# A block of two networks on one core: first projection in three passes of rounded parts, convolution taps spread over the stage and the heads of retention

## The reference, cut to what matters

```python
h = _rmsnorm(x, norm_g[0, 0]) * (1.0 + scale_m) + shift_m     # mod = silu(c) @ ada_w + ada_b
proj = h @ w_in                                                # (256, 1024) @ (1024, 3072)
a_val, a_gate, q, k, v, g = split(proj)                        # six parts of 512 columns
a = a_val * sigmoid(a_gate)
a = depthwise_conv(a, conv_w)                                  # 31 taps, 512 channels
a = silu(_layernorm(a + conv_b, cln_g, cln_b))
q, k = _rotary(q), _rotary(k)
r = silu(g) * _head_rmsnorm(_retention_bidir(q, k, v))         # 4 heads of 128
mix = concatenate([a, r]) @ w_out
```

## Time and profile before

| | us |
|---|---|
| median of 3 runs | 1404.34 (1403.9 to 1406.63) |
| the profiled execution | 1400.26 |
| its span in the profile | 1398.5 |

### The profile page before, as it was taken

The page is one execution under the profiler, slowest core; times in us unless marked ns, Lnnn a source line. Parts: engine busy times, 40 slices in busy tenths (PEclk is TensorE's granted clock), DMA queues, the critical chain, the costliest instruction groups (busy, mean ns, idle before and its releaser), DMA issues.

```text
span 1398.5 us, 21667 instructions
## 1 busy us (share of the span) xinstructions
PE 1208.0 (86%) x9250; PEld 1070.8 (77%) x9250; DVE 784.0 (56%) x1328; ACT 518.7 (37%) x857; POOL 164.5 (12%) x129
## 2 busy tenths in 40 slices
PE   5899888879979998658999999788798799887797
PEld 3688566668868887357899999788786698776697
DVE  1177312875554466775566543489776445467545
ACT  2112312211210006424455534434465535357634
POOL 0111100100000000010000000156454100041000
PEclk8999989989989998868899999889998799998899
DMA  9977659658866883899455556234332054342141
GB/s 294 354 250 242 212 125 264 208 191 279 315 228 216 150 289 114 288 248 137 136 179 184 183 192 194 65 103 135 112 105 91 31 190 142 94 131 78 61 136 45
DMA packets 203204, 244.36 MB, mean 175 GB/s; under 512 B 27173, under 2 KB 187557, under 8 KB 198885
## 3 DMA queue, kind: packets, MB, share of 16 engines
q1 hardware_dynamic: 187528, 182.24, 42.8%
q0 software_dynamic: 11280, 42.78, 10.3%
q10 hardware_dynamic: 4300, 17.96, 3.3%
HBM read 224.16 MB, written 18.81 MB: 174 GB/s over the span
## 4 chain that ended last, share of the span: by engine, by line
PE 65%; DVE 17%; DMA 6%; ACT 5%; SPq 3%; issue 3%; ACTq 0%; POOL 0%; DVEq 0%
PE ps L1285 17%; PE ps L1278 10%; PE ps L1280 10%; PE ps L1282 10%; PE ps L1333 2%; DVE ada_w L2353 2%; PE ps L1363 2%; PE ps L1306 2%; DMA ring<-in_w_glu_b 1%; DMA ada_w<-in_ada_w 1%; SPq L684 1%; PE ps L1699 1%; PE ps L1767 1%; DVE ring_rounded L1889 1%; DMA more<-in_ada_w 1%
## 5 line engine op out<-in xcount | busy, mean ns | idle before, releaser
L1278 PE MATMUL ps<-sq_rounded,w_high_rounded 128*128 128x256 f32 x960 | 283.6, 295 | 27.4 <-DVE ring_rounded L1889 8.8
L1282 PE MATMUL ps<-sq_rounded,ring_rounded 128*128 128x256 f32 x960 | 276.4, 288 | 0.0
L1280 PE MATMUL ps<-hT_rounded,w_high_rounded 128*128 128x256 f32 x832 | 239.0, 287 | 0.0
L1889 DVE TENSOR_TENSOR ring_rounded<-ring,w_high_rounded 128x1024 fp32r<-128x1024 f32 x152 | 186.6, 1270 | 88.2 <-ACT w_high_rounded L811 88.1
L1278 PEld LDWEIGHTS ps<-sq_rounded,w_high_rounded 128*128 128x128 f32 x960 | 190.1, 198 | 37.9 <-issue 31.3
L811 ACT ACTIVATE w_high_rounded<-ring 128x1024 fp32r<-128x1024 f32 x176 | 175.9, 1049 | 101.4 <-PE ps L1282 95.0
L1285 PE MATMUL ps<-hT,ring 128*128 128x256 f32 x832 | 188.3, 385 | 5.9 <-ACT hT L876 3.2
L1282 PEld LDWEIGHTS ps<-sq_rounded,ring_rounded 128*128 128x128 f32 x960 | 189.4, 197 | 0.0
L1285 PEld LDWEIGHTS ps<-hT,ring 128*128 128x128 f32 x832 | 157.7, 192 | 34.6 <-issue 13.3
L1280 PEld LDWEIGHTS ps<-hT_rounded,w_high_rounded 128*128 128x128 f32 x832 | 164.2, 197 | 0.3
L1278 PE MATMUL ps<-more_rounded,w_high_rounded 128*128 128x256 f32 x448 | 126.0, 281 | 1.6 <-issue 1.4
(11 more groups left out here) (377 smaller groups left out, 1829.1 us busy)
## 6 DMA issues: line engine op xcount, KB each, us to landing
ring<-in_w_fc SPq DMA_DIRECT2D x64, 1024.0 KB, 5.5
ada_w<-in_ada_w POOLq DMA_DIRECT2D x27, 1024.0 KB, 7.7
ring<-in_ssm_in_w SPq DMA_DIRECT2D x20, 1024.0 KB, 5.3
ada_more<-in_ada_w POOLq DMA_DIRECT2D x13, 1024.0 KB, 7.7
ring<-in_w_in SPq DMA_DIRECT2D x12, 1024.0 KB, 8.1
we_dram<-we_t ACTq DMA_DIRECT2D x8, 1024.0 KB, 5.5
ca_dram<-more ACTq DMA_DIRECT2D x8, 1024.0 KB, 8.0
ring<-we_dram SPq DMA_DIRECT2D x8, 1024.0 KB, 4.9
```

Source lines behind the costliest of these rows:

```text
L1278: nc.tensor.matmul(out, high[:, k, columns], x_high, start=start, stop=False, skip_group_check=True)
L1280: nc.tensor.matmul(out, high[:, k, columns], x_low, start=False, stop=False, skip_group_check=True)
L1282: last = nc.tensor.matmul(out, low[:, k, columns], x_high, start=False, stop=stop, skip_group_check=True)
L1889: nc.vector.tensor_tensor(rounded(w), w, w_high[:, c % 2, ks], ALU.subtract)\
```

## The change

The first projection joins the split phases. ACT rounds and DVE lowers each of its twelve blocks; the shift is folded into the split of the activations (ACT writes the rounded part to sq, DVE the rest to hT, in the helper `split_shifted`, which is taken over from phase fc1_1); blocks 8 and 9 get a form of their own, `project_tokens_split`, which waits for both halves of the lowered block. ACT rounds block 0, and DVE lowers it, ahead of the norm. DVE's taps are cut up: of 31, the first 24 are spread three at a time over eight turns of a loop that first lowers a block and in turns 1 to 4 also rotates; the last seven (LATE_TAPS) stand behind the decays of the four heads, 1, 2, 2 and 2. Counters of later waits are moved accordingly. The hunks with those counters alone are left out here.

```diff
@@ -51,6 +51,7 @@
 NCH = T // L
 WIN = (2 * L - 1) * GC
 PI = 3.1415925
+LATE_TAPS = 7
 S5_AT_FC1 = (1, 4, 7, 10, 13)
 MODULATION_AT_FC1 = (7,)
 SINGLE = 1.5 * 2 ** 23
@@ -176,11 +177,11 @@
 
 
 
-SPLIT_LO = {"glu": "vector", "fc1_1": "vector", "fc2_1": "vector", "xbc": "gpsimd", "z": "vector",
+SPLIT_LO = {"w_in": "vector", "glu": "vector", "fc1_1": "vector", "fc2_1": "vector", "xbc": "gpsimd", "z": "vector",
             "ssm_out": "vector", "ple_gate_0": "vector", "q": "vector", "gate": "vector",
             "attn_out": "vector", "ple_gate_1": "vector"}
 
-SPLIT_SETS = (("glu", 4), ("fc1_1", 8), ("fc2_1", 16), ("xbc", 8), ("ssm_out", 16), ("ple_gate_0", 8), ("q", 8),
+SPLIT_SETS = (("w_in", 8), ("glu", 4), ("fc1_1", 8), ("fc2_1", 16), ("xbc", 8), ("ssm_out", 16), ("ple_gate_0", 8), ("q", 8),
               ("attn_out", 8), ("ple_gate_1", 8))
 SET_BASE = {name: sum(n for _, n in SPLIT_SETS[:i]) for i, (name, _) in enumerate(SPLIT_SETS)}
 
@@ -805,7 +806,10 @@
                     c = split_next[0]
                     b = split_order[c]
                     act.wait_ge(w_here[b % RING], here[b])
-                    act.wait_ge(blocks_done, split_order[c - 2] + 1 if c >= 2 else first_block["glu"] - 2 * (1 - c))
+                    if b in (first_block["glu"], first_block["glu"] + 1):
+                        act.wait_ge(blocks_done, b - 2 + b - first_block["glu"])
+                    elif c >= 2:
+                        act.wait_ge(blocks_done, split_order[c - 2] + 1)
                     for half in range(2):
                         ks = slice(4 * half, 4 * half + 4)
                         nc.scalar.activation(w_high[:, c % 2, ks], ring[:, b % RING, ks], ACT.Copy)\
@@ -889,7 +893,10 @@
             for p in range(PIECES // 2):
                 act.wait_ge(ada0_parts, p + 1)
                 nc.scalar.activation(mix_flat[:, 512 * p:512 * p + 512], PS[p][:, :], ACT.Copy).then_inc(ada0_copied, 1)
-            shift(0, 0, SHIFT_M)
+            round_to(first_block["w_in"] + 1)
+            for k in range(DT):
+                act.wait_ge(hn_ready, k + 1)
+                round_tiles(sq[:, k], hT[:, k], mod(0, SHIFT_M, k))
 
 
             for j in range(2):
@@ -1305,6 +1312,22 @@
                     for k in range(KB):
                         last = nc.tensor.matmul(ps[:, i], lhs[:, k, P * i:P * i + P], w[:, k],
                                                 start=(k == 0), stop=(k == KB - 1))
+                last.then_inc(blocks_done, 1)
+
+            def project_tokens_split(phase, n, x_high, x_low):
+
+                ps = pair(start_unit(phase, n))
+                b = first_block[phase] + n
+                high, low = w_high[:, split_place[b] % 2], rounded(ring[:, b % RING])
+                pe.wait_ge(w_low_vector, 2 * split_low[b][1])
+                for i in range(TT):
+                    for k in range(KB):
+                        t_high, t_low = (rounded(x[:, k, P * i:P * i + P]) for x in (x_high, x_low))
+                        nc.tensor.matmul(ps[:, i], t_high, high[:, k], start=(k == 0), stop=False,
+                                         skip_group_check=True)
+                        nc.tensor.matmul(ps[:, i], t_high, low[:, k], start=False, stop=False, skip_group_check=True)
+                        last = nc.tensor.matmul(ps[:, i], t_low, high[:, k], start=False, stop=(k == KB - 1),
+                                                skip_group_check=True)
                 last.then_inc(blocks_done, 1)
 
             def project_deep(phase, n, kblocks, x, arrived=None):
@@ -1398,18 +1421,18 @@
 
 
             def h_arrived(i):
-                return lambda k: pe.wait_ge(h_ready, 8 * i + k + 1)
+                return lambda k: pe.wait_ge(h_ready, 8 * (i - 1) + k + 1)
 
             pe.wait_ge(x_ready, 4)
             pe.wait_ge(tables_here, 32)
             for n in range(8):
-                project("w_in", n, (hT,), h_arrived(0) if n == 0 else None)
+                project("w_in", n, (sq, hT), split_arrived("w_in") if n == 0 else None)
                 modulation(PIECES + n)
             for n in range(8, 10):
-                project_tokens("w_in", n, hT)
+                project_tokens_split("w_in", n, sq, hT)
                 modulation(PIECES + n)
             for n in range(10, 12):
-                project("w_in", n, (hT,))
+                project("w_in", n, (sq, hT))
                 modulation(PIECES + n)
 
...
@@ -1950,17 +1973,33 @@
                                                              op0=ALU.mult, op1=ALU.add)
                     ins.then_inc(x_ready, 1)
 
+            def split_shifted(phase, i, layer, which):
+                dve.wait_ge(rstd_ready, i + 1)
+                for k in range(DT + 2):
+                    if k < DT:
+                        nc.vector.scalar_tensor_tensor(out=hT[:, k], in0=xT[:, k], scalar=gains[:, i, k:k + 1],
+                                                       in1=rstd[:, :], op0=ALU.mult, op1=ALU.mult).then_inc(hn_ready, 1)
+                    if k >= 2:
+                        j = k - 2
+                        dve.wait_ge(a_high, SET_BASE[phase] + j + 1)
+                        nc.vector.scalar_tensor_tensor(out=rounded(hT[:, j]), in0=hT[:, j],
+                                                       scalar=mod(layer, which, j), in1=rounded(sq[:, j]),
+                                                       op0=ALU.add, op1=ALU.subtract).then_inc(a_low, 1)
+
+            lower_to(first_block["w_in"] + 1)
             modulation(0)
             gain(0)
-            normed(0, lambda k: gains[:, 0, k:k + 1])
+            split_shifted("w_in", 0, 0, SHIFT_M)
 
 
             nc.vector.memset(apad[:, :, 0:PAD], 0.0)
             nc.vector.memset(apad[:, :, PAD + T:], 0.0)
             for j in range(2):
+                lower_to(first_block["w_in"] + 2 * j + 2)
                 dve.wait_ge(sg_ready, j + 1)
                 ps = unit("w_in", 2 * j + 1)
                 nc.vector.tensor_tensor(apad[:, 2 * j:2 * j + 2, PAD:PAD + T], ps, sgate, ALU.mult).then_inc(a_ready, 1)
+                lower_to(first_block["w_in"] + 2 * j + 3)
             dve.wait_ge(a_ready, 2)
 
             def taps(first, last):
@@ -1990,10 +2029,12 @@
                 link(nc.vector.tensor_tensor(b, b, table("rope_sin").unsqueeze(1).to_broadcast([P, 2, T]), ALU.mult))
                 nc.vector.tensor_tensor(a, a, b, ALU.add).then_inc(qk_ready, 1)
 
-            taps(0, 14)
-            for j in range(4):
-                rotate(j)
-            taps(14, TAPS)
+            early = TAPS - LATE_TAPS
+            for n in range(8):
+                lower_to(first_block["w_in"] + n + 6)
+                taps(early * n // 8, early * (n + 1) // 8)
+                if 1 <= n <= 4:
+                    rotate(n - 1)
 
 
             def decayed(h):
@@ -2015,6 +2056,7 @@
 
             for h in range(HEADS):
                 decayed(h)
+                taps(early + LATE_TAPS * h // HEADS, early + LATE_TAPS * (h + 1) // HEADS)
                 if h >= 1:
                     gated(h - 1)
...
@@ -2273,16 +2315,7 @@
                     ins = nc.vector.scalar_tensor_tensor(out=xT[:, k], in0=glu_prod[:, i], scalar=mod(1, GATE_M, k),
                                                          in1=xT[:, k], op0=ALU.mult, op1=ALU.add)
                 ins.then_inc(x_ready, 1)
-            dve.wait_ge(rstd_ready, 4)
-            for k in range(DT + 2):
-                if k < DT:
-                    nc.vector.scalar_tensor_tensor(out=hT[:, k], in0=xT[:, k], scalar=gains[:, 3, k:k + 1],
-                                                   in1=rstd[:, :], op0=ALU.mult, op1=ALU.mult).then_inc(hn_ready, 1)
-                if k >= 2:
-                    j = k - 2
-                    dve.wait_ge(a_high, SET_BASE["fc1_1"] + j + 1)
-                    nc.vector.scalar_tensor_tensor(out=rounded(hT[:, j]), in0=hT[:, j], scalar=mod(1, SHIFT_F, j),
-                                                   in1=rounded(sq[:, j]), op0=ALU.add, op1=ALU.subtract).then_inc(a_low, 1)
+            split_shifted("fc1_1", 3, 1, SHIFT_F)
             for n in range(17):
                 if n < 16:
                     lower_to(first_block["fc1_1"] + n + 2)
```

More of the change, by code:

```diff
@@ L1558, in _ @@
                         if jq == 0:
-                            pe.wait_ge(h_ready, 8 * 2 + k + 1)
+                            pe.wait_ge(h_ready, 8 + k + 1)
                         last = nc.tensor.transpose(PS[2 * kh + jq][:, P * i:P * i + P],
@@ L2212, in _ @@
                 if b == 0:
-                    dve.wait_ge(h_ready, 8 * 3)
+                    dve.wait_ge(h_ready, 8 * 2)
                 nc.vector.tensor_copy(u_in[:, 16 * b:16 * b + 16].rearrange("p g s -> p (g s)"), PS[b][:, :])\
```

## The result

The changed kernel takes 1419.07 us, median of 4 runs (1414.76 to 1426.88), against 1404.12 before: the ratio is 1.0122, 95% interval 1.0088 to 1.0156. It is slower, as forecast, but by 15 us in the medians and 17 by the ratio, three to four times the 4.35 us of the sum, and outside the range.

The account below looks back on a forecast made before the run. PE was taken to bound the first projection, with DVE taking over after the change; +0.6 us at retention's entry and +3.7 in the heads gave +4.35, 1404.6 profiled or 1408.7 by the median, range 1403 to 1413.5.

Parts of the forecast that it names:

- Part 3: First projection: ACT's order makes PE wait 2.7 us before blocks 2 and 4; block 4 starts 5.3 us late.
- Part 5: Retention heads: five late taps on DVE's path add 3.7 us; past that point nothing is changed.
- Part 1: First projection's passes: a block loses 1.51 us on PE, 18.1 over twelve, against 28.3 more on DVE.
- Part 2: Start of the first projection: block 0 waits for DVE's low parts; block 1 starts at 59.6, 4.3 us later.
- Block 0 is quick: Rival, 12%: block 0's matmuls after the last low part take 2.15 us less; +2.2 us, 1406.5.
- Part 4: First projection from block 5: DVE's list sets the pace, one 0.2 us wait for ACT; retention starts at 150.0, 0.6 late.
- one of the signs that I had named for being wrong: Wrong if DVE idles between 90 and 150, blocks 2 and 4 start unwaited, or PE ends projection well before 140.
- The falling clock: Rival, 19%: clock falls in new waits, 1.7 us each, and in heads and pieces; up to +7.6, 1416, likelier 1412.5.

Follow-up runs that it names:

- after_order: The changed kernel with ACT rounding blocks 2 and 4 one modulation row earlier; ratio 1.0019 to the kernel before, median 1405.92 us.
- after_late0: The changed kernel with all 31 taps in the first projection, none between the heads; one execution, 1416.98 us.
- after_fc: The changed kernel with the first weight load of fc1_0 issued ahead of SP's list of small loads; ratio 1.0078 to the kernel before, median 1416.66 us.
- after_tail: The changed kernel with the seven late taps dealt 1, 1, 1, 4 over the heads; one execution, 1404.57 us.
- after_warm: The changed kernel with unread constant matmuls in PE's waits before blocks 2 and 4, in heads and pieces; ratio 1.0062 to the kernel before, median 1408.92 us.
- after_again: The changed kernel, unedited, executed once more; 1415.08 us.
- before_again: The kernel before the change, unedited, executed once more; 1402.42 us.
- mended_late10: The changed kernel with earlier rounding of blocks 2 and 4, earlier fc1_0 load, added matmuls, ten late taps (1, 1, 1, 7); ratio 0.9890, median 1385.11 us.
- pool_warm: pool_tail with unread constant matmuls behind pieces 20 to 22 and both LayerNorm statistics; ratio 0.9967 to the kernel before.
- pool_tail: The changed kernel with POOL lowering blocks 5, 7, 9, 11, earlier ACT rounding, late taps 1, 1, 1, 4, earlier fc1_0 load; ratio 1.0029 to the kernel before.

## Why the prediction was wrong

Two steps failed. Part 3 ended its sum at the two waits and put nothing for PE's slower work behind them. Part 5 took everything behind the heads for unchanged. The numbers follow, part by part.

**Part 1, right, and not where the time went.** Blocks run at 0.12 us a matmul wherever the clock is up, and DVE's loop of 8.96 us hides it.

**Part 2, right in kind, 1.8 us too much.** Block 1 starts at 57.8, not 59.6. The lowering, the norm and the low parts ended at 53.1 against 53.3. From there PE needed 3.6 us to the end of block 0, not 5.3, since the clock rose at the last low part here and 3.3 us behind it in fc1_1. I had carried over a size that hangs on when the clock rises. The rival *Block 0 is quick* (12%) was right on this point, with 1.8 of its 2.15 us.

**Part 3, right on the waits, wrong on their price.** The waits were 2.84 and 2.93 us against 2.7. The sum stopped at the wait. The fall of the clock behind it stood only as a rival, at 1.7 us each; measured were 2.7 us in block 2 (8.45 against 5.8) and 1.4 in block 4 (7.2, from 87.66 to 94.86), and after_order showed the order's whole price at the entry: 10.0 us, not 5.5. A wait that thins PE was costed without PE's slower work behind it. That is the first of the two steps that failed.

**Part 4, right in kind, one wait mis-sized.** DVE sets the pace from block 5 on; seven more taps cost 10.5 us in after_late0. But it waited 2.02 us for ACT's rounding of block 6, not 0.2, and so met one of the signs that I had named for being wrong, idle time of DVE between 90 and 150. ACT rounds that block behind block 4's copies, and the first part of block 4 ran at the low clock. Where all of it ran at the high clock (after_fc, after_tail, after_warm) the wait was 0.7 us. The entry came at 152.7 instead of 150.0: 1.6 us from block 4's late start, 1.8 from this wait, with 0.7 taken back since the list itself was shorter. So most of it is part 3's low clock, net of the 1.8 us that part 2 had given back.

**Part 5, the heads right in part by luck, what follows wrong.** 15.56 us from the entry to piece 20 against a forecast of 12.8 + 2.8 = 15.6. Two misses cancel in that: up to the end of the last decay it took 12.25 us, 0.55 less than forecast, DVE's pace hiding PE's low clock; behind it PE took 3.3 us instead of 2.78. And "past that point nothing is changed" was the second step that failed. Pieces 20 to 23 took 12.96 us instead of 9.41, all of them at a granted clock of 0.50; in after_warm, after_tail and after_late0, at 1.00, they took 9.58, 9.02 and 9.02.

**The rest.** The 7.6 us behind w_out of the profiled execution stood in no case of mine. In after_again, with a list of 29 us, 2.0 of them are left (0.6 up to the block and 1.4 in it, against before_again); the rest belongs to the one execution. Why the list takes 29 us in one execution and 37 in another I did not find, and it was not tried to take the list away. Nor is it known how many of the four timed executions had the long one, so of the 17 us by the ratio only the pair's 12.5 are accounted for.

**The rivals.** The falling clock was the case that happened. I gave it 19%, too little by what the traces held: the earlier trace rows already had a fall behind a wait of 2.60 us, and the change puts two waits of that size and a thinned retention into the path. It was priced at up to +7.6 above the forecast, 12 in all, which is close to what the pair without the long list shows (12.5); its terms were 3.4 us for the two blocks (measured 4.1), 1.5 for the heads (0.5) and 2.7 for the pieces (3.6). The rule of the Trainium skill's page Perfetto Trace Analysis, section Identifying the Most-Contended Engine, to optimize the engine with the highest occupancy first, did not hold for this change: from block 5 on the less busy DVE set the pace (67.36 us of 95 against PE's 86.02). In mended_late10, with DVE's list cut, less work on PE did pay. The 0.424 us of the Trainium skill's page VectorE: DVE Perf Modes, section on the TRN2 errata, is above the distance of back-to-back taps again: 24 take 9.59 us, 0.40 each. A single fp32 operation of two tensors of this size takes 0.42 us (DVE L2054 in the changed kernel), which agrees with the page.

## What to carry to other kernels

When a change takes work off PE, cost the clock with it: a wait of 2.8 us in front of a block cost here up to as much again behind it, and the low clock reached pieces of work that the change had not touched. Put such a fall down with a chance, since the same wait had none in another execution. When an engine's list serves another one's next block, put that step ahead of any wait for the block in hand; one line of order was worth 10 us here. Work that must only be done by a later point belongs behind the last step that others wait for, not evenly between them.

## What the runs showed of the hardware

Added matmuls that nobody reads made a kernel faster: pool_warm against pool_tail, 0.9967 to 1.0029. In the LayerNorm's stretch of all five kernels that had them the granted clock was 1.00, and w_out's first block took 7.14 us instead of 9.60. Behind waits of one length the clock fell in some executions and not in others: behind 2.84 us in front of block 2 it fell in four profiles and stayed at 1.00 in after_tail. In the changed kernel PE was busy 3.43 of 4 us with pieces of the modulation, and the granted clock stayed at 0.50, the 1.2 GHz level:

```profile
170.00:174.00 4.00, 3.43 (x32) 1.65 (x24) 0.38 (x1) 0.45 (x2) 0.89 (x1) 0.50 0.13 30
```

In the kernel before the same pieces, entered at the high clock, left PE idle a third of the time and ran at 1.00:

```profile
161.20:169.00 7.80, 5.36 (x65) 3.24 (x64) 0.85 (x2) 2.23 (x8) 2.66 (x3) 1.00 0.50 158
```

In before_again it fell on the way through them (0.76 over 9.96 us), with the same code.

The list of 18 small loads on SP took 37 us in one execution of the changed kernel and 29 in another. Of the nine profiles in which it stands ahead of the weight load of fc1_0, seven have 29 to 30 us and two have 37; in all eight in which it stands behind that load it took 35 to 39 us.
